# Down tiles of both feed-forward loops in halves of 64 rows, on both halves of TensorE's array by turns

## What is computed

```python
# first block, D_FF = 2816
gate, up = jnp.split(h @ w_gate_up, 2, axis=-1)
x = x + (jax.nn.silu(gate) * up) @ w_down
# second block, D_FF_2 = 4096
u = jax.nn.relu(h @ w_ff1)
y = (u * u) @ w_ff2
```

## Time and profile before

| | |
|---|---|
| three executions | 749.6, 749.85, 750.36 us; median 749.85 |
| profiled execution: span | 747.8 us |
| what lies around the span, against the median | 2.05 us |
| TensorE busy in the span | 733.6 us (98%) |
| VectorE, ScalarE busy | 538.5 us (72%), 377.7 us (51%) |
| first layer, first start of the first of its 8 down tiles here to the end of the last | 180.89 to 305.22 us |
| second layer, the same for its 13 | 583.70 to 723.81 us |

### The profile page before, as it was taken

The page is one execution under the profiler, slowest core; times in us unless marked ns, Lnnn a source line. Parts: engine busy times, 40 slices in busy tenths (PEclk is TensorE's granted clock), DMA queues, the critical chain, the costliest instruction groups (busy, mean ns, idle before and its releaser), DMA issues.

```text
span 747.8 us, 13134 instructions
## 1 busy us (share of the span) xinstructions
PE 733.6 (98%) x5288; PEld 676.5 (90%) x5288; DVE 538.5 (72%) x927; ACT 377.7 (51%) x544; POOL 51.1 (7%) x72
## 2 busy tenths in 40 slices
PE   7999999999999999999999999999999999999996
PEld 7999987789999999998999999999988998998995
DVE  6798798586677776847669978884967876555554
ACT  7434778664433334446444447665645445445442
POOL 1950000000000000000432000000000000000000
PEclk9999999999999999999999999999999999999999
DMA  8736421478787888642354556554733674644611
GB/s 327 238 121 237 159 66 49 163 305 334 293 319 294 306 322 316 236 163 89 132 196 148 175 201 250 202 187 170 276 118 113 249 258 170 224 168 168 224 57 57
DMA packets 27022, 151.10 MB, mean 202 GB/s; under 512 B 3128, under 2 KB 7836, under 8 KB 9564
## 3 DMA queue, kind: packets, MB, share of 16 engines
q1 hardware_dynamic: 22620, 124.81, 46.0%
q10 hardware_dynamic: 3456, 25.17, 8.5%
q0 software_dynamic: 896, 0.43, 0.3%
HBM read 148.92 MB, written 1.05 MB: 201 GB/s over the span
## 4 chain that ended last, share of the span: by engine, by line
PE 81%; DVE 12%; ACT 3%; DMA 2%; issue 1%; SPq 0%; DVEq 0%; ACTq 0%
PE ps L468 24%; PE ps L469 24%; PE ps L470 24%; DVE ada L1763 4%; DVE w_lo L1667 2%; PE ps L791 2%; DMA raw<-wts 2%; PE ps L589 1%; PE ps L1041 1%; ACT w_hi L1220 1%; DVE w_lo L1740 1%; PE ps L623 1%; PE ps L613 1%; PE ps L641 1%; PE ps L1027 1%
## 5 line engine op out<-in xcount | busy, mean ns | idle before, releaser
L1667 DVE TENSOR_TENSOR w_lo<-raw,w_hi 128x2048 fp32r<-128x2048 f32 (+2 forms) x105 | 237.6, 2268 | 111.9 <-ACT w_hi L1220 111.7
L468 PE MATMUL ps<-h_hi,w_hi 128*128 128x256 f32 (+2 forms) x1000 | 284.7, 285 | 1.1 <-DVE h_lo L1719 1.1
L469 PE MATMUL ps<-h_lo,w_hi 128*128 128x256 f32 (+2 forms) x1000 | 282.8, 283 | 0.0
L470 PE MATMUL ps<-h_hi,w_lo 128*128 128x256 f32 (+2 forms) x1000 | 282.8, 283 | 0.0
L1220 ACT CAST w_hi<-raw 128x2048 fp32r<-128x2048 f32 (+2 forms) x105 | 196.9, 1887 | 50.4 <-PE ps L470 46.5
L468 PEld LDWEIGHTS ps<-h_hi,w_hi 128*128 128x128 f32 (+2 forms) x1000 | 190.2, 190 | 3.4 <-issue 2.3
L469 PEld LDWEIGHTS ps<-h_lo,w_hi 128*128 128x128 f32 (+2 forms) x1000 | 190.3, 190 | 1.2
L470 PEld LDWEIGHTS ps<-h_hi,w_lo 128*128 128x128 f32 (+2 forms) x1000 | 190.2, 190 | 0.3
L468 PE MATMUL ps<-w_hi,mix_hi 128*128 128x512 f32 x248 | 97.4, 393 | 0.4 <-DVE w_lo L1667 0.2
L469 PE MATMUL ps<-w_lo,mix_hi 128*128 128x512 f32 x248 | 96.8, 390 | 0.0
L470 PE MATMUL ps<-w_hi,mix_lo 128*128 128x512 f32 x248 | 96.5, 389 | 0.0
(11 more groups left out here) (313 smaller groups left out, 906.0 us busy)
## 6 DMA issues: line engine op xcount, KB each, us to landing
raw<-wts SPq DMA_DIRECT2D x109, 1024.0 KB, 4.8
ada<-w_ada ACTq DMA_DIRECT2D x24, 1024.0 KB, 5.2
alibi<-wts SPq DMA_DIRECT2D x2, 1024.0 KB, 6.9
fa_whole<-wts SPq DMA_DIRECT2D x2, 1024.0 KB, 6.2
resid<-x SPq DMA_DIRECT2D x2, 512.0 KB, 4.1
raw<-wts SPq DMA_DIRECT2D x2, 512.0 KB, 6.6
rows_ga<-rows_wide SPq DMA_DIRECT2D x1, 1024.0 KB, 6.7
out<-resid SPq DMA_DIRECT2D x4, 256.0 KB, 2.0
```

The costliest lines, as they stand in the source:

```text
L468: nc.tensor.matmul(o, lh, rh, start=start, stop=False)
L469: nc.tensor.matmul(o, lh, rl, start=False, stop=False)
L470: return nc.tensor.matmul(o, ll, rh, start=False, stop=stop)
L1667: V.tensor_tensor(w_lo[:, s % RING, 0:w], raw[:, n_of[name] % RAW, 0:w], w_hi[:, s % RING, 0:w].bitcast(F32), ALU.subtract).then_inc(w_rea ...
```

## The change

A new function `half_rows` takes the place of `acc_tile` (through `down`) in `ff1_step` and in the loop's `ff2_step`. Each product of 128 rows becomes two products of 64 rows, one on the partitions 0 to 63, the other on 64 to 127 (`rs`), both 512 columns wide. The two that stand next to each other in the list go to different output banks (`n = b ^ ph`): in phase 0 the lower rows to n = 0 and the upper rows to n = 1, in phase 1 the other way round. A tile is four such phases (tokens m = 0 and 1 with phase 0, then m = 0 and 1 with phase 1) of 12 products. Phase 1 of each m waits until phase 0 of the same m is complete (a new semaphore, `row_phase`, in the profile `half_rows_phase`), since it adds to the same two banks from the other half of the array. Before a tile there is one more wait, for the down tile before (`pe_tile`). The rest of the program, and what the other engines do, stays as it was.

```diff
+            def acc_phase(slot, hi, lo, m, ph, first):
+
+                wh, wl = w3(slot, 2)
+                ms = slice(m * P, (m + 1) * P)
+                for kk in range(2):
+                    for at, (h, w) in enumerate(((hi, wh), (hi, wl), (lo, wh))):
+                        for b in range(2):
+                            n = b ^ ph
+                            rs = slice(b * HD, (b + 1) * HD)
+                            i = nc.tensor.matmul(ps[:, 2 * m + n, :], h[rs, kk, ms], w[rs, kk, n * 512:(n + 1) * 512],
+                                                 start=first and ph == 0 and (kk, at) == (0, 0), stop=False)
+                return i
+
+            def half_rows(slot, hi, lo, first, phases):
+
+                for m in range(2):
+                    acc_phase(slot, hi, lo, m, 0, first).then_inc(row_phase, 1)
+                for m in range(2):
+                    pe.wait_ge(row_phase, phases + m + 1)
+                    i = acc_phase(slot, hi, lo, m, 1, first)
+                return i
...
-            def down(slot, buf, first, last):
-                return acc_tile(slot, hid_hi[buf], hid_lo[buf], 0, first, last)
...
-                    down((s0 + 2) % RING, (st - 1) % 2, first, False).then_inc(pe_tile, 1)
+                    if st > 1:
+                        pe.wait_ge(pe_tile, i * 6 + (s_idx[f"down{st - 2}"] + 1))
+                    buf = (st - 1) % 2
+                    half_rows((s0 + 2) % RING, hid_hi[buf], hid_lo[buf], first, i * 4 + 2 * (st - 1)).then_inc(pe_tile, 1)
...
-                down((s0 + 1) % RING, (st - 1) % 3, False, False).then_inc(pe_tile, 1)
+                pe.wait_ge(pe_tile, i * 6 + (s_idx[f"fb{st - 2}"] + 1))
+                buf = (st - 1) % 3
+                half_rows((s0 + 1) % RING, hid_hi[buf], hid_lo[buf], False, i * 6 + 2 * (FF1_STEPS - 3) + 2 * (st - 2)).then_inc(pe_tile, 1)
```

More of the change, by code:

```diff
@@ L285, in build @@
         s_va = [sem(f"va{i}_landed") for i in range(2)]
+        row_phase = sem("half_rows_phase")
         rows_first = sem("third_quarter_complete")
```

## The result

The changed kernel takes 757.97 us (median of 4 runs, 757.48 to 758.78), the kernel before 749.73 us in the same comparison (4 runs, 749.35 to 750.36). The ratio is 1.0109, with a 95% interval of 1.0095 to 1.0123: 8.2 us slower, where 8.3 us were forecast. The span of the profiled execution grew from 747.8 to 755.7 us.

What follows compares the result with a forecast made beforehand. TensorE was taken to bound the kernel; 24 pairs at 0.228 us plus 0.39 us for switching made each of 21 tiles 0.39 us longer, +8.3 us on 749.85, 758.2 us, with an 8-in-10 range of 751 to 767 us.

Steps and rivals of the forecast that it cites:

- What bounds the kernel: Whole kernel: TensorE busy 733.6 of 747.8 us, without slack in both layers' stretches, so down-tile changes count one for one.
- P: Price of a pair of 64-row products in a down tile: 0.228 us, the same as one 128-row product today.
- rival 4: Down tiles: fp32r halves don't run side by side, +5.9 us a tile, 873 us; chance 0.04.
- Rival 1: Down tiles: the other half covers the swap, P = 0.216 us, +0.11 us a tile, 752.2 us; chance 0.20.
- S: Price of going over to halves and back, once for each of 21 down tiles: 0.39 us, 8.2 us in all.
- Rival 2: Down tiles: going over is cheaper, S 0.19 us with P 0.216, kernel faster at 747.8 us; chance 0.14.
- The waits: Three per down tile, for `pe_tile` and ahead of each phase 1: costed at nothing, being covered by the other phase.
- rival 3: Down tiles: each product pays the fixed part (764.1 us) or the phase waits bite (766.6 us); chance 0.13.
- The sum: Per down tile 24 x 0.228 + 0.39 = 5.86 us against 5.47; 21 tiles give +8.3 us, 758.2 us.

Runs made afterwards that it cites:

- stays of 8 pairs, one and two of them: Against the changed kernel, only one or two groups of 8 pairs per tile in halves, the other products whole: 759.0 us with one, 767.82 us with two.
- Turns in threes: The changed kernel with three products of the lower 64 rows listed, then three of the upper, and so on: 758.23 us in one run.
- runs of six: The changed kernel with each phase listed as six products of the lower rows, then six of the upper: 771.13 us in one run.
- runs of twelve: The changed kernel with twelve lower-row products, then twelve upper per phase of both m, and one uncovered wait: 849.01 us in one run.
- bare wait above: The changed kernel with each m's phase 1 right behind its phase 0, so nothing covers the two waits: 773.73 us, ratio 1.0321.

## Why the prediction was right, step by step

- **What bounds the kernel.** TensorE had no slack in both stretches, and the loss came out one for one: 21 x 0.38 = 8.0 us by the windows, 7.9 in the span, 8.2 in the time.
- **P.** Forecast 0.228 us for a pair, measured 0.227. That fp32r halves run side by side at full rate, into two banks at once, was carried over from float32 rows at half the rate, with rival 4 as the case against it; the changed kernel shows it. Rival 1 (0.216, the other half covers the swap) is refuted: the 0.011 us over the price of the columns are there in each pair as in each whole product. By the Trainium skill's rule that loads overlap only where row groups differ (TensorE: Matmul & The Clock Gate, Part 3) it would have come. Both traces disagree with that rule: loads of all 128 rows start with a product of all 128 (597.44 beside 597.44 in the earlier trace rows), and loads of both halves start 0.01 us behind a pair that holds both (601.24 and 601.23).
- **S.** Forecast 0.39 us (0.395 in the sum), measured 0.38, with the same four parts at the same four starts. That it is paid per stay, and not per pair, is shown by the stays of 8 pairs, one and two of them. Rival 2 needed it below 0.28.
- **The waits.** Costed at nothing, and they are nothing in the changed kernel. What they would cost without cover I took from S and had too low, 0.2 for 0.38 us: a wait on the array's own product has the report in it as well. It touched only the bound of rival 3, whose 8.4 us for 42 bare waits should have been 15.8.
- **The sum.** 5.86 us a tile were forecast; the two windows give 11.60 - 5.75 = 5.85. The number is right by its terms, and not by luck: P and S were each measured within 0.01 us of the forecast, and neither makes up for an error of the other.

What wasn't settled: why a product pays the 0.011 us that don't grow with its columns, and what the array does in each of the four parts of S. No run here takes them apart.

## What to carry to other kernels

Splitting a product that already fills all 128 rows into halves saves no column time: each half streams the same columns, so the price of a pair is that of the whole product, and going over to halves and back costs 0.38 to 0.43 us each time. By the float32 rows and these pairs, halves pay only for products that are really 64 rows deep, and then in as few stays as the program allows, with enough other work listed between a phase and the wait for it: here 0.45 us passed from the phase's last start to the next. Before such a change, look in the trace for any place that already makes the switch, and take the difference between its starts and those of its neighbours: both terms of this sum stood there.

## What the runs showed of the hardware

- The array takes a product of one half ahead of up to three waiting ones of the other. Turns in threes are as good as turns one by one (5.67 and 5.66 us for a tile); runs of six take 6.33 us, runs of twelve 9.98 us.
- The first products of 512 columns behind a restart or behind narrower ones are dearer. In the kernel with one stay of 8 pairs the first five steps of a tile take 1.16 us (599.16 to 600.32), 0.232 us each, and the next ten 2.26 us (600.32 to 602.58), 0.226 each. Behind the bare wait above the steps take 0.232 us too. Each stay amid products of 512 columns pays this once more, about 0.03 us by these rows, and so makes up the greater part of the difference between 0.38 and 0.43 us. Its cause wasn't looked for. The timeline of that kernel, the first, the sixth and the last whole product of a tile:

```profile
599.16 0.40 PE L544 MATMUL ps<-w_hi,mix_hi 128*128 128x512 f32 x1
...
600.32 0.39 PE L544 MATMUL ps<-w_lo,mix_hi 128*128 128x512 f32 x1
...
602.58 0.39 PE L544 MATMUL ps<-w_lo,mix_hi 128*128 128x512 f32 x1
```
